# A decoder step on one Trainium2 core: one ones-matmul moved by one key tile, and the token operands of the mixing stage moved ahead on two engines

## The chip, the cores and the metric

The kernel runs on one core of one Trainium2 chip. A core has five engines with a queue of instructions each: TensorE (PE, matrix products, with its weight loads shown apart as PEld), VectorE (DVE), ScalarE (ACT), GpSimd (POOL) and SyncE (SP); here SP and POOL only issue transfers. The engines meet through semaphores. The metric is the device time of one execution in microseconds (us).

## The reference, cut to what matters

One layer of a decoder over 512 prompt tokens and 32 sample tokens (544 columns in the kernel), width 2048. Only the start of it is touched: the keys and values of 256 memory rows, and the normalised tokens that go into the combined projection `w_in`.

```python
def _rms(x, g):
    xf = x.astype(jnp.float32)
    y = xf * lax.rsqrt(jnp.mean(xf * xf, axis=-1, keepdims=True) + EPS)
    return (y * g.astype(jnp.float32)).astype(x.dtype)

def _mem_kv(mem, g_mem, w_k, w_v):
    m = _rms(mem, g_mem)
    k = (m @ w_k).reshape(Bn, N_MEM, N_XHEADS, XHEAD_DIM)
    v = (m @ w_v).reshape(Bn, N_MEM, N_XHEADS, XHEAD_DIM)
    return k, v
...
    h = _rms(x, norm_mix)
    proj = h @ w_in
    u = proj[..., :POOL_WIDTH]
...
```

Behind it come pooling and convolution, an output projection, cross-attention to the memory, a squared-ReLU MLP and a final normalisation.

## The kernel before

The order of the work is written out by hand, an instruction list for each engine. Every fp32 product is made of three products of rounded parts: an operand is rounded by ACT to its high part, DVE subtracts that from the original to get the low part, and PE adds high x high, high x low and low x high.

Weights come in **units** of 128 x 1024, through a ring of four slots. Unit n is loaded by SP into `unit_raw` as soon as DVE has split unit n-4 (L489), rounded by ACT into `unit_high` (L790, `convert`) when PE has used unit n-4, and split by DVE into `unit_low` (L1310, `convert`); PE waits for that split. So both converting engines run up to four units ahead of PE, and no further.

The stages around the change:

- **Key tiles** (L2165, `key_tile` on PE): 16 tiles of 128 key columns, t = 0 to 15, two units each, k0 to k31. DVE scales each finished tile into `temp` (L1382) and POOL stores it (L602). Beside them the tokens `residual` are squared: ACT makes the square (L804), DVE adds it to `square_sums` (L1320), one or two of the 16 slices beside each of the tiles 0 to 11, by the table `X_BY_KEY`. The code of DVE and ACT for tile t also converts units 2t+8 and 2t+9 of the run of k and v units, which wait for PE to use units 2t+4 and 2t+5: they run ahead of PE by those.
- **The sum of squares** (L2221, `sum_squares` on PE): four matmuls with a matrix of ones, when all 16 slices have been added. Before, it stands behind key tile 13 (`j == 1` of the last group of four, the 14th of the 16). From it DVE and ACT make `rstd` (`rstd_tokens`: L1326, the root on ACT L799, then three DVE steps L1331 to L1333).
- **Value units** (L2276): v0 to v31, twelve matmuls of 512 columns each. The loop number m = 0 to 27 in the code of ACT and DVE converts unit v(m+4). After v7, v15, v23 and v31 DVE scales two results (L1564).
- **Token operands**: the 16 slices of the tokens are handled in eight pairs, k = 0 to 7. For one pair DVE normalises two slices (L1434, `normalise_in`), ACT rounds their first halves (L850, `high_first`), DVE makes their low parts (L1405, `low_tokens`) and four sums and differences (`mix_tokens`, L1412 to L1420), ACT rounds two of these (`high_mixed`) and DVE makes the low parts (`low_mixed`). Before, the pairs stand beside the value units at m = 1, 4, 7, ..., 22, a whole pair at a time, with the mixed part of a pair one step later.
- **The combined projection** (L2300, `product_in`): 16 quads of seven products each, made of sums of weight blocks. The four blocks of quad 0 go into the ring's slots as v28 to v31 are split (SP, L501 to L507); DVE adds them (L1451, L1456, L1460, L1464), ACT rounds (L885), DVE splits (L1442). PE's product i of a quad waits, for i = 5, until ACT has copied partial result 3 (`copy_in`, L889).

Of the kernel before, what the change touches and what calls it, by code (L numbers as in the profile page):

```python
# [26 lines left out]
KT = D // P  # L27
# [4 lines left out]
CH = 8  # L32
# [53 lines left out]
START, TOTAL = starts()  # L86
# [102 lines left out]
def build(nc, weights, x_t, mem_t, params, cache_k, cache_v, pool_state, conv_state,  # L189
          y_t, k_t, v_out, pool_new, conv_new):  # L190
    ctx = ExitStack()
    with ctx:
# [592 lines left out]
        def _(act):  # L785
# [11 lines left out]
            def root(n, source, out):  # L797
                act.wait_ge(var_ready, n + 1)
                act.activation(out[:, 0:source.shape[1]], source, ACT.Abs_reciprocal_sqrt).then_inc(root_ready, 1)  # L799
# [39 lines left out]
            for t in range(KT):  # L839
# [4 lines left out]
                if t < KT - 2:  # L844
                    for n in (4, 5):
                        convert_next(unit("k_proj", 0, 2 * t + n))
            root(1, RSTD[:, :], ROOT_Y)

            def high_tokens(turn, i, k, source):
                act.activation(X7[i][:, k, 0, :], source, ACT.Copy).then_inc(tok_high[i], 1)  # L850
# [6 lines left out]
            def high_mixed(turn, k):  # L857

                for i, n in ((3, 1), (2, 3)):
                    act.wait_ge(tok_mixed, 4 * CH * turn + 4 * k + n)  # L860
                    high_tokens(turn, i, k, X7RAW[i][:, k, 1, :])
# [60 lines left out]
            def first_tap(g, r):  # L922
# [9 lines left out]
                act.activation(by_row(Y[:, c, SEQ:TOK]), own(Z[:, r, :], CPAD)[:, :, 0:DEC], ACT.Identity, scale=tap) \  # L932
                    .then_inc(tapped, 1)

            for i in range(4):
                for n in range(8):
                    m = 8 * i + n
                    if m < 28:
                        convert_next(unit("v_proj", 2 * i, n))
                    if m % 3 == 1 and m < 25:  # L940
                        k = m // 3
                        for p in (2 * k, 2 * k + 1):
                            high_first(MIX, p)
                        if k:
                            high_mixed(MIX, k - 1)
                    if m == 25:
                        high_mixed(MIX, CH - 1)
                    if m in (29, 30):
                        high_in(0, m - 29)
            high_in(0, 2)  # L950
# [352 lines left out]
        def _(dve):  # L1303
# [73 lines left out]
            def key_tile(t):  # L1377
                if t >= 2:

                    dve.wait_ge(k_stored[t % 2], 16 * (t // 2))  # L1380
                product(unit("k_proj", 0, 2 * t + 1))
                dve.tensor_tensor((TC, TD)[t % 2][:, 0:MEM], M[:, t % 4, 0:MEM], RSTDM[:, 0:MEM], ALU.mult) \  # L1382
                    .then_inc(psum_free, 1)
                if t == 0:
                    convert_next(unit("k_proj", 0, 3))
                for x in X_BY_KEY[t]:
                    add_squares(x, x + s0["squares"], SUMS, TOK)
                if t < KT - 2:
                    for n in (4, 5):
                        convert_next(unit("k_proj", 0, 2 * t + n))  # L1390

            for t in range(KT):
                key_tile(t)
            rstd_tokens(1, START["v_proj"]["squares"], ROOT_Y, ROOT_Z)

            for j in range(2):
                dve.wait_ge(k_stored[j], 16 * KT // 2)


            def b_block(j, l, k):  # L1400
                return X[:, CH * j + k, l * HALF:l * HALF + HALF]

# [29 lines left out]
            def normalise_in(p):  # L1432
                t = ORDER[p]
                dve.scalar_tensor_tensor(X[:, t, :], X[:, t, :], PAR[:, G_MIX + t:G_MIX + t + 1], RSTD[:, :],  # L1434
                                         ALU.mult, ALU.mult).then_inc(tok_normal, 1)

            def low_in(q, i):

# [116 lines left out]
            for i in range(4):  # L1555
                for n in range(8):
                    m = 8 * i + n
                    if n == 7:
                        product(unit("v_proj", 2 * i, 7))
                        for j in range(2):  # L1560
                            if i:

                                dve.wait_ge(v_stored[j], 16 * i)
                            dve.tensor_scalar((TC, TD)[j][:, 0:512], M[:, 2 * (i % 2) + j, 0:512],  # L1564
                                              RSTDM[:, MEM + j:MEM + j + 1], None, ALU.mult).then_inc(v_staged, 1)
                    if m < 28:
                        convert_next(unit("v_proj", 2 * i, n))
                    if m % 3 == 1 and m < 25:
                        k = m // 3
                        normalise_in(2 * k)  # L1570
                        normalise_in(2 * k + 1)
                        if k:
                            low_mixed(MIX, k - 1)
                        low_tokens(MIX, 0, k, k + 1, b_block(0, 0, k))
                        low_tokens(MIX, 1, k, k + 1, b_block(1, 0, k))
                        mix_tokens(MIX, k)
                    if m == 25:
                        low_mixed(MIX, CH - 1)
                    if m == 29:
                        sum_in_1(0)  # L1580
                        low_in(0, 0)
                    if m == 30:
                        sum_in_3(0)
                        low_in(0, 1)
                        sum_in_2(0)
# [571 lines left out]
        def _(pe):  # L2157
# [104 lines left out]
                    key_tile(i, j, False)  # L2262
            for j in range(4):
                key_tile(KT // 4 - 1, j, False)
                if j == 1:
                    sum_squares(1, START["v_proj"]["squares"])


# [494 lines left out]
```

## Time and profile before

| | us |
|---|---|
| median of 3 runs (lowest, highest) | 2620.81 (2619.9, 2622.91) |
| the profiled execution | 2623.57 |
| its span in the profile | 2621.9 |
| PE busy | 2573.2 (98%) |
| DVE busy | 1913.5 (73%) |
| ACT busy | 1105.8 (42%) |

The profiled execution is 2.76 us above the median; 1.67 us of it lie outside the span. The rows shown further below are times in that span. A timeline row gives the start in us, the duration, the engine, the line, the operation, what it writes and reads, how many were merged, and in brackets how long the engine sat idle before it and for whom. The row of a chain is a start, a duration and what ran.

### The profile page before, as it was taken

The page shows a single profiled execution, that of the slowest core. Times are in us where ns is not written, and L with a number is a line of the kernel's source. Part 1 is how long each engine was busy: PE and PEld are TensorE (multiplying, and loading weights), DVE is VectorE, ACT ScalarE, POOL GpSimd, SP SyncE. Part 2 cuts the span into 40 slices and gives each one's busy share as a digit, 9 for nine tenths or more (in the row PEclk, how much of TensorE's full clock was granted, in tenths as well). Part 3 has the DMA queues.
Part 4 walks back from the last instruction along what each step waited for, and adds up shares of the span by engine and source line. Part 5 has one row for each costly group of instructions (what it writes and reads, how often), then busy time and mean ns, then how long its engine had stood idle before and what let it go on. Part 6 is the DMA issues. An engine that isn't in the chain of part 4 may idle for free.

```text
span 2621.9 us, 47591 instructions
## 1 busy us (share of the span) xinstructions
PE 2573.2 (98%) x20056; PEld 2515.4 (96%) x20056; DVE 1913.5 (73%) x2342; ACT 1105.8 (42%) x1520; POOL 159.9 (6%) x253
## 2 busy tenths in 40 slices
PE   8999999999999999999999999999999999999997
PEld 8979999999999989989999999999999999999997
DVE  6688888773542244368988888888887888888888
ACT  6444444451331122134656555555543333333344
POOL 1000000010000000000011110000010000000000
PEclk9999999999999999999999999999999999999999
DMA  8653333362233445533466666555587555556542
GB/s 281 214 195 115 112 110 111 114 208 89 88 107 126 153 181 195 196 122 114 155 221 218 216 220 219 194 208 200 201 288 288 183 199 182 193 195 210 192 140 101
DMA packets 131856, 462.51 MB, mean 176 GB/s; under 512 B 11952, under 2 KB 18224, under 8 KB 120400
## 3 DMA queue, kind: packets, MB, share of 16 engines
q1 hardware_dynamic: 92448, 260.05, 30.3%
q0 software_dynamic: 39216, 199.71, 20.6%
q8 instruction: 144, 2.36, 0.4%
q14 instruction: 48, 0.39, 0.0%
HBM read 376.62 MB, written 83.09 MB: 175 GB/s over the span
## 4 chain that ended last, share of the span: by engine, by line
PE 88%; DVE 6%; issue 2%; ACT 2%; DMA 1%; SPq 0%; DVEq 0%; POOL 0%; ACTq 0%; POOLq 0%
PE psum_main L2555 27%; PE psum_main L2165 25%; PE psum_side L2555 20%; PE psum_main L2300 6%; PE psum_side L2300 4%; DVE unit_low L1310 1%; PE psum_main L2409 1%; PE psum_main L2481 1%; DVE unit_low L1843 1%; PE psum_side L2450 1%; PE psum_side L2374 1%; PE psum_main L2276 1%; DVE unit_low L1442 1%; DMA unit_raw<-weights 1%; DVE tokens L1405 0%
## 5 line engine op out<-in xcount | busy, mean ns | idle before, releaser
L1155 ACT ACTIVATE unit_high<-unit_raw 128x1024 fp32r<-128x1024 f32 x384 | 400.7, 1055 | 532.2 <-PE psum_main L2555 158.3
L1843 DVE TENSOR_TENSOR unit_low<-unit_raw,unit_high 128x1024 fp32r<-128x1024 f32 x384 | 468.1, 1222 | 109.1 <-ACT unit_high L1155 108.9
L2555 PE MATMUL psum_main<-tokens,unit_high 128*128 128x272 f32 x2048 | 388.5, 288 | 4.3 <-DVE hidden L1946 3.3
L2555 PE MATMUL psum_main<-hidden,unit_high 128*128 128x272 f32 x1984 | 377.1, 288 | 4.0 <-DVE residual L1976 2.7
L2165 PE MATMUL psum_main<-inner_a,unit_high 128*128 128x272 f32 x2080 | 348.1, 289 | 0.6 <-issue 0.6
L790 ACT ACTIVATE unit_high<-unit_raw 128x1024 fp32r<-128x1024 f32 x162 | 169.6, 1056 | 420.2 <-PE psum_main L2165 403.8
L2555 PEld LDWEIGHTS psum_main<-tokens,unit_high 128*128 128x128 f32 x2048 | 321.8, 189 | 5.2 <-DVE hidden L1946 4.0
L2555 PEld LDWEIGHTS psum_main<-hidden,unit_high 128*128 128x128 f32 x1984 | 312.2, 189 | 5.1 <-DVE residual L1976 3.7
L2165 PEld LDWEIGHTS psum_main<-inner_a,unit_high 128*128 128x128 f32 x2080 | 294.3, 188 | 3.8 <-issue 3.6
L2555 PE MATMUL psum_main<-tokens,unit_low 128*128 128x272 f32 x1024 | 295.0, 288 | 0.0
L2555 PE MATMUL psum_side<-tokens,unit_high 128*128 128x272 f32 x1536 | 293.1, 288 | 1.4 <-issue 0.8
L1310 DVE TENSOR_TENSOR unit_low<-unit_raw,unit_high 128x1024 fp32r<-128x1024 f32 x162 | 196.6, 1223 | 127.3 <-ACT unit_high L790 126.5
L2555 PE MATMUL psum_main<-hidden,unit_low 128*128 128x272 f32 x992 | 286.1, 288 | 0.0
L2555 PE MATMUL psum_side<-hidden,unit_high 128*128 128x272 f32 x1488 | 283.7, 288 | 0.2 <-DVE unit_low L1843 0.2
L2555 PEld LDWEIGHTS psum_side<-tokens,unit_high 128*128 128x128 f32 x1536 | 242.0, 189 | 2.0 <-issue 1.2
L2555 PEld LDWEIGHTS psum_side<-hidden,unit_high 128*128 128x128 f32 x1488 | 234.3, 189 | 0.6 <-issue 0.6
L2555 PE MATMUL psum_side<-tokens,unit_low 128*128 128x272 f32 x768 | 221.6, 288 | 0.0
L2165 PE MATMUL psum_main<-inner_a,unit_low 128*128 128x272 f32 x1040 | 214.7, 287 | 0.0
L2555 PE MATMUL psum_side<-hidden,unit_low 128*128 128x272 f32 x744 | 214.5, 288 | 0.0
L2300 PE MATMUL psum_main<-tokens,unit_high 128*128 128x272 f32 x1024 | 194.7, 288 | 4.0 <-DVE conv_gates L1486 4.0
L2555 PEld LDWEIGHTS psum_main<-tokens,unit_low 128*128 128x128 f32 x1024 | 192.4, 188 | 0.0
L2555 PEld LDWEIGHTS psum_main<-hidden,unit_low 128*128 128x128 f32 x992 | 186.4, 188 | 0.0
(285 smaller groups left out, 4699.0 us busy)
## 6 DMA issues: line engine op xcount, KB each, us to landing
unit_raw<-weights SPq DMA_DIRECT2D x442, 512.0 KB, 4.3
hidden<-hidden_kept POOLq DMA_DIRECT2D x56, 1088.0 KB, 6.2
hidden_kept<-hidden_staged POOLq DMA_DIRECT2D x31, 1904.0 KB, 7.4
unit_sum<-weights SPq DMA_DIRECT2D x40, 512.0 KB, 3.6
residual<-x_t POOLq DMA_DIRECT2D x16, 544.0 KB, 6.5
residual_kept<-residual POOLq DMA_DIRECT2D x32, 272.0 KB, 5.0
cache_ring_t<-cache_k POOLq DMA_DIRECT2D x8, 1024.0 KB, 7.8
cache_low_a<-cache_v POOLq DMA_DIRECT2D x8, 1024.0 KB, 10.6
```

What stands on the lines that cost most here:

```text
L790: act.activation(WHI[:, s, :], RAW[:, s, :], ACT.Copy).then_inc(high_ready, 1)
L1155: act.activation(WHI[:, slot, :], raw, ACT.Copy).then_inc(mlp_high, 1)
L1310: dve.tensor_tensor(WLO[:, s, :], RAW[:, s, :], WHI[:, s, :].bitcast(F32), ALU.subtract) \
L1442: dve.tensor_tensor(WLO[:, slot, :], raw, WHI[:, slot, :].bitcast(F32), ALU.subtract) \
L1843: dve.tensor_tensor(WLO[:, slot, :], raw, WHI[:, slot, :].bitcast(F32), ALU.subtract) \
L2165: ins = pe.matmul(out, weights_at(w), moving, start=first and n == 0, stop=last and n == len(passes) - 1)
L2276: ins = pe.matmul(M[:, 2 * i + mt, 0:512], MEMS[:, 2 * n + kk, part, mt * P:mt * P + P], w[:, u[1], kk * 512:kk * 512 + 512], start=(n + k ...
L2300: ins = pe.matmul(out, w[:, slot, cols], X7[i][:, k, part, :], start=start and k == 0 and n == 0, stop=k == CH - 1 and n == 2, skip_group_ ...
L2374: ins = pe.matmul(S[32 * j:32 * j + 32, 2 + h % 2, r * MEM:r * MEM + MEM], Q[:, HT * h + k, SEQ:TOK], key_place(at)[:, j, kk * MEM:kk * ME ...
L2409: ins = pe.matmul(M[:, p % 4, 0:MEM], Q[:, HT * h + dk, tt * P:tt * P + P], keys, start=dk == 0, stop=dk == HT - 1)
L2450: ins = pe.matmul(S[32 * i:32 * i + 32, 2 + r, :], PS[:, mt, r, 32 * i:32 * i + 32], value_place(g, m)[:, i, :], start=mt == 0, stop=mt == 1)
L2555: ins = pe.matmul(bank, w[:, slot, col:col + P], moving[:, k, part, :], start=start and k == 0 and n == 0, stop=k == kk - 1 and n == 2, sk ...
```

## The change

Three edits.

1. PE: the sum of squares stands behind key tile 12 (`j == 0`) instead of key tile 13.
2. DVE: `rstd` is made behind the code of key tile 13 instead of behind tile 15. Pair 0 follows the scaling of tile 14, pair 1 that of tile 15, both ahead of the conversion of v4. ACT: the roundings of pairs 0 and 1 stand ahead of the conversion of v4.
3. The pairs 2 to 7 stand at m = 0, 4, ..., 20 in two portions: normalising and the mixed low parts of the pair before at m, the low parts and `mix_tokens` at m + 2. On ACT the pair's rounding is at m. Pair 7's mixed part is at m = 24.

The diff's core:

```diff
@@ ACT
             for t in range(KT):
...
-            root(1, RSTD[:, :], ROOT_Y)
+                if t == KT - 3:
+                    root(1, RSTD[:, :], ROOT_Y)
...
+            for p in (0, 1):
+                high_first(MIX, p)
+            high_mixed(MIX, 0)
+            for p in (2, 3):
+                high_first(MIX, p)
             for i in range(4):
                 for n in range(8):
                     m = 8 * i + n
                     if m < 28:
                         convert_next(unit("v_proj", 2 * i, n))
-                    if m % 3 == 1 and m < 25:
-                        k = m // 3
+                    if m % 4 == 0 and m < 28:
+                        high_mixed(MIX, m // 4 + 1)
+                    if m % 4 == 0 and m < 24:
+                        k = m // 4 + 2
                         for p in (2 * k, 2 * k + 1):
                             high_first(MIX, p)
-                        if k:
-                            high_mixed(MIX, k - 1)
-                    if m == 25:
-                        high_mixed(MIX, CH - 1)
@@ DVE
+            def first_operands(k):
+                low_tokens(MIX, 0, k, k + 1, b_block(0, 0, k))
+                low_tokens(MIX, 1, k, k + 1, b_block(1, 0, k))
+                mix_tokens(MIX, k)
+
             for t in range(KT):
                 key_tile(t)
-            rstd_tokens(1, START["v_proj"]["squares"], ROOT_Y, ROOT_Z)
+                if t == KT - 3:
+                    rstd_tokens(1, START["v_proj"]["squares"], ROOT_Y, ROOT_Z)
+                if t >= KT - 2:
+                    k = t - (KT - 2)
+                    normalise_in(2 * k)
+                    normalise_in(2 * k + 1)
+                    if k:
+                        low_mixed(MIX, k - 1)
+                    first_operands(k)
...
-                    if m % 3 == 1 and m < 25:
-                        k = m // 3
+                    k = m // 4 + 2
+                    if m % 4 == 0 and m < 24:
                         normalise_in(2 * k)
                         normalise_in(2 * k + 1)
-                        if k:
-                            low_mixed(MIX, k - 1)
-                        low_tokens(MIX, 0, k, k + 1, b_block(0, 0, k))
-                        low_tokens(MIX, 1, k, k + 1, b_block(1, 0, k))
-                        mix_tokens(MIX, k)
-                    if m == 25:
+                        low_mixed(MIX, k - 1)
+                    if m % 4 == 2 and m < 24:
+                        first_operands(k)
+                    if m == 24:
                         low_mixed(MIX, CH - 1)
@@ PE
             for j in range(4):
                 key_tile(KT // 4 - 1, j, False)
-                if j == 1:
+                if j == 0:
                     sum_squares(1, START["v_proj"]["squares"])
```

What stands in a row on DVE around the start of the value units. The names: `unit_low` is a unit's split, `temp_64` and `temp_65` take key tiles with even and odd number, the lines have moved by a few. Before, from the last two splits of the key tiles' code (v2 and v3) on:

```order
L1310 TENSOR_TENSOR unit_low<-unit_raw,unit_high 128x1024 [waits high_ready] x2
L1382 TENSOR_TENSOR temp_64<-psum_main,rstd_mem 128x256 [waits units_used,k_stored_0]
L1382 TENSOR_TENSOR temp_65<-psum_main,rstd_mem 128x256 [waits units_used,k_stored_1]
L1326 TENSOR_SCALAR rstd<-psum_side 128x544 [waits sums_done,summed]
L1331 TENSOR_TENSOR root_z<-root_y 128x544 [waits root_ready,var_ready]
L1332 SCALAR_TENSOR_TENSOR root_z<-root_z,rstd 128x544 [waits dve_steps]
L1333 SCALAR_TENSOR_TENSOR rstd<-root_z,root_y 128x544 [waits dve_steps]
L1310 TENSOR_TENSOR unit_low<-unit_raw,unit_high 128x1024 [waits k_stored_1,high_ready,k_stored_0,dve_steps]
L1310 TENSOR_TENSOR unit_low<-unit_raw,unit_high 128x1024 [waits high_ready]
L1434 SCALAR_TENSOR_TENSOR residual<-residual,par,rstd 128x544 x2
L1405 TENSOR_TENSOR tokens_90<-residual,tokens_90 128x272 [waits tok_high_0]
```

Now, from the scaling of key tile 15 on (pair 0, from L1430 to L1416, stands ahead of it):

```order
L1386 TENSOR_TENSOR temp_65<-psum_main,rstd_mem 128x256 [waits units_used,k_stored_1]
L1430 SCALAR_TENSOR_TENSOR residual<-residual,par,rstd 128x544 x2
L1401 TENSOR_TENSOR tokens_93<-tokens_raw_100,tokens_93 128x272 [waits tok_high_3]
L1401 TENSOR_TENSOR tokens_92<-tokens_raw_99,tokens_92 128x272 [waits tok_high_2]
L1401 TENSOR_TENSOR tokens_90<-residual,tokens_90 128x272 [waits tok_high_0]
L1401 TENSOR_TENSOR tokens_91<-residual,tokens_91 128x272 [waits tok_high_1]
L1408 TENSOR_TENSOR tokens_raw_100<-residual 128x272 [waits tok_normal]
L1409 TENSOR_TENSOR residual<-residual 128x272
L1412 SCALAR_TENSOR_TENSOR tokens_raw_99<-residual 128x272 [waits tok_mixed]
L1416 SCALAR_TENSOR_TENSOR residual<-tokens_raw_99,residual 128x272 [waits tok_ready_1,tok_mixed]
L1314 TENSOR_TENSOR unit_low<-unit_raw,unit_high 128x1024 [waits high_ready,k_stored_1,k_stored_0]
L1430 SCALAR_TENSOR_TENSOR residual<-residual,par,rstd 128x544 x2
```

The split of v4 (the `unit_low` row that waits for both `k_stored`) stood ahead of every pair; now two pairs stand ahead of it.

On ACT, behind the root, before:

```order
L799 ACTIVATE root_y<-rstd 128x544 [waits var_ready]
L790 ACTIVATE unit_high<-unit_raw 128x1024 [waits raw_loaded_0,units_used]
L790 ACTIVATE unit_high<-unit_raw 128x1024 [waits raw_loaded_1,units_used]
L850 ACTIVATE tokens_90<-residual 128x272 [waits tok_normal]
L850 ACTIVATE tokens_91<-residual 128x272 [waits tok_normal]
```

and now:

```order
L799 ACTIVATE root_y<-rstd 128x544 [waits var_ready]
L851 ACTIVATE tokens_90<-residual 128x272 [waits tok_normal]
L851 ACTIVATE tokens_91<-residual 128x272 [waits tok_normal]
L851 ACTIVATE tokens_93<-tokens_raw_100 128x272 [waits tok_mixed]
L851 ACTIVATE tokens_92<-tokens_raw_99 128x272 [waits tok_mixed]
L851 ACTIVATE tokens_90<-residual 128x272 [waits tok_normal]
L851 ACTIVATE tokens_91<-residual 128x272 [waits tok_normal]
L790 ACTIVATE unit_high<-unit_raw 128x1024 [waits raw_loaded_0,units_used]
L851 ACTIVATE tokens_93<-tokens_raw_100 128x272 [waits tok_mixed]
L851 ACTIVATE tokens_92<-tokens_raw_99 128x272 [waits tok_mixed]
L851 ACTIVATE tokens_90<-residual 128x272 [waits tok_normal]
L851 ACTIVATE tokens_91<-residual 128x272 [waits tok_normal]
```

Six roundings that wait for DVE's pairs 0 and 1 have moved ahead of the rounding of v4, and the four behind it ahead of that of v5.

## Rows read from the trace of the kernel before

**Rows 1.** One stretch, the value units: start:end, length, busy us of each engine, clock, DMA.
```profile
110.50:204.50 94.00, 88.89 (x386) 71.50 (x385) 78.91 (x124) 43.15 (x64) 4.33 (x8) 1.00 0.56 189
```

**Rows 2.** Waits from 88 to 230 us: who waited for whom, total, times, longest.
```profile
PE psum_main L2276 <- DVE unit_low L1310: 5.1, 6, 1.6
...
PE psum_side L2300 <- ACT partial_in L889: 2.7, 1, 2.7
```

**Rows 3.** Chain of waits, 85 to 112 us: key tiles 14 and 15 on PE.
```profile
99.20 11.52 PE psum_main L2165 x96
```

**Rows 4.** Timeline, 92 to 99 us, engines mixed: tile 12's end, the last square, the sum.
```profile
92.56 1.06 ACT L790 ACTIVATE unit_high<-unit_raw 128x1024 fp32r<-128x1024 f32 x1 [1.82 <-PE psum_main L2165]
...
93.65 1.23 DVE L1310 TENSOR_TENSOR unit_low<-unit_raw,unit_high 128x1024 fp32r<-128x1024 f32 x1 [1.66 <-ACT unit_high L790]
...
95.13 0.72 DVE L1320 TENSOR_TENSOR square_sums<-square_sums,temp 128x544 f32<-128x544 f32 x1
...
98.12 1.08 PE L2221 MATMUL psum_side<-square_sums,par 128*128 128x272 f32 x4
```

**Rows 5.** Timeline, PE's first value matmul, then DVE up to v6's split.
```profile
110.54 0.40 PE L2276 MATMUL psum_main<-unit_high,mem_split 128*128 128x512 f32 x1
...
113.64 0.71 DVE L1326 TENSOR_SCALAR rstd<-psum_side 128x544 f32<-128x544 f32 x1
...
116.67 0.72 DVE L1333 SCALAR_TENSOR_TENSOR rstd<-root_z,root_y 128x544 f32<-128x544 f32 x1
117.89 2.36 DVE L1310 TENSOR_TENSOR unit_low<-unit_raw,unit_high 128x1024 fp32r<-128x1024 f32 x2 [0.49 <-DMA k_t<-temp]
120.17 1.47 DVE L1434 SCALAR_TENSOR_TENSOR residual<-residual,par,rstd 128x544 f32<-128x544 f32 x2
...
124.15 3.49 DVE L1310 TENSOR_TENSOR unit_low<-unit_raw,unit_high 128x1024 fp32r<-128x1024 f32 x3
```

**Rows 6.** Timeline, ACT, behind the second rounding of pair 0.
```profile
122.01 2.00 ACT L790 ACTIVATE unit_high<-unit_raw 128x1024 fp32r<-128x1024 f32 x2
```

**Rows 7.** Timeline, DVE, one whole pair (k = 3) between splits.
```profile
146.42 1.47 DVE L1434 SCALAR_TENSOR_TENSOR residual<-residual,par,rstd 128x544 f32<-128x544 f32 x2
148.72 0.79 DVE L1405 TENSOR_TENSOR tokens<-tokens_raw,tokens 128x272 fp32r<-128x272 f32 x2 [0.82 <-ACT tokens L850]
...
151.79 3.49 DVE L1310 TENSOR_TENSOR unit_low<-unit_raw,unit_high 128x1024 fp32r<-128x1024 f32 x3
```

**Rows 8.** Timeline: v23's scaling on DVE, v27's start and quad 0's on PE.
```profile
188.20 1.40 DVE L1564 TENSOR_SCALAR temp<-psum_main,rstd_mem 128x512 f32<-128x512 f32 x2
...
190.79 0.50 PE L2276 MATMUL psum_main<-unit_high,mem_split 128*128 128x512 f32 x1 [1.56 <-DVE unit_low L1310]
...
204.52 0.47 PE L2300 MATMUL psum_main<-tokens,unit_high 128*128 128x272 f32 x2
```

**Rows 9.** Timeline, DVE and SP, from v31's split to quad 0's first sum.
```profile
196.12 1.23 DVE L1310 TENSOR_TENSOR unit_low<-unit_raw,unit_high 128x1024 fp32r<-128x1024 f32 x1 [1.27 <-ACT unit_high L790]
197.37 0.33 SPq L507 DMA_DIRECT2D unit_raw<-weights  x1
...
202.04 1.22 DVE L1451 TENSOR_TENSOR unit_sum<-unit_raw 128x1024 f32<-128x1024 f32 x1 [4.70 <-DMA unit_raw<-weights]
```

**Rows 10.** Chain of waits, 203 to 232 us: quad 0's product 1, then products 4's end to 5.
```profile
207.74 3.01 PE psum_side L2300 x24
...
220.05 2.09 ACT tokens L850 x2
...
222.48 4.67 PE psum_side L2300 x24
```

**Rows 11.** Stretches, columns as rows 1: behind that wait, and from 1920 us.
```profile
222.20:225.60 3.40, 3.12 (x14) 3.12 (x15) 3.27 (x4) 2.12 (x3) 0.00 (x0) 0.50 0.51 154
...
1920.00:1924.00 4.00, 3.15 (x24) 2.92 (x24) 1.05 (x1) 1.06 (x1) 0.53 (x1) 1.00 1.05 391
```

**Rows 12.** Timeline, PE: the longest wait behind which the clock stayed full.
```profile
1919.88 0.52 PE L2555 MATMUL psum_main<-tokens,unit_high 128*128 128x272 f32 x2 [2.29 <-DVE hidden L1946]
```

More of the change, by code:

```diff
@@ L1390, in key_tile @@
                         convert_next(unit("k_proj", 0, 2 * t + n))
-            for t in range(KT):
-                key_tile(t)
-            rstd_tokens(1, START["v_proj"]["squares"], ROOT_Y, ROOT_Z)
-            for j in range(2):
-                dve.wait_ge(k_stored[j], 16 * KT // 2)
             def b_block(j, l, k):
@@ L1435, in normalise_in @@
                                          ALU.mult, ALU.mult).then_inc(tok_normal, 1)
+            def first_operands(k):
+                low_tokens(MIX, 0, k, k + 1, b_block(0, 0, k))
+                low_tokens(MIX, 1, k, k + 1, b_block(1, 0, k))
+                mix_tokens(MIX, k)
+            for t in range(KT):
+                key_tile(t)
+                if t == KT - 3:
[7 more added lines that the diff above has]
+                    first_operands(k)
+            for j in range(2):
+                dve.wait_ge(k_stored[j], 16 * KT // 2)
             def low_in(q, i):
```

## The prediction

> **What bounds the kernel now.** I read the table of busy times first: PE is busy 98% of the span, so the time is PE's work and its pauses, and an edit counts only where PE waits or where the clock of its array falls. Then the waits of PE beside the changed code. There are two kinds [rows 2]: six waits of the value units for DVE's splits, 5.1 us, and one wait of quad 0's product 5 for ACT, 2.7 us. Third, the stretch of the value units [rows 1]: of 94.0 us PE is busy 88.9 and DVE 78.9. DVE holds PE up there because its work comes in lumps. A pair takes DVE from 146.42 to 151.79 = 5.4 us, and the three splits that follow 3 x 1.14 = 3.4 (the spacing of the two splits that start at 117.89 and end for the pair at 120.17), together 8.8 [rows 5, 7]. PE needs three units in that time. One unit is 2.72 us: five of them run from 190.79 to 204.52, 13.73 us, of which a restart takes 0.1 [rows 8]. Three are 8.2, so DVE loses 0.6 us to PE at each pair, and PE pays once its lead is used up. The whole stage runs from 110.54 to 204.52, 94.0 us, against 32 x 2.72 = 87.0 of matmuls: 6.9 us are lost (5.1 as idle time, the rest as restarts and pipeline refill).
>
> **Edit 1, the sum of squares one tile earlier.** It is worth nothing where it is used: DVE takes it up at 113.64 [rows 5], 14 us after the matmuls at 98.12 [rows 4], because DVE comes to `rstd` only behind the split of v3, which waits for PE's last key unit. The edit puts `rstd` behind key tile 13's code, but that code ends with this very split, so it only jumps two scalings (0.33 us each).
> Its cost is a new wait. PE's sum waits until all 16 squares are added. Two key tiles take 11.52 us, one 5.76 [rows 3]. The sum starts at 98.12 behind tile 13, so tile 12 ends at 98.12 - 5.76 = 92.36. The last square is added at 95.13 + 0.72 = 95.85 [rows 4]. Can it come sooner? On DVE it stands behind a split that waits for ACT, and ACT's rounding waited for PE to finish tile 12 (92.56, released by PE) [rows 4]: rounding, split, the scaling of tile 11, the addition, a chain of 3.5 us that only starts when PE reaches the sum. So PE stands from 92.36 to about 95.9, **+3.5 us**. Before, tile 13 covered this chain. Behind the waiting sum stand tiles 13 to 15 and everything else on PE; nothing that DVE holds then can catch up for it, since PE is the bound there. Bounds: 3.4 and 3.7, it is read off four rows.
>
> **The clock behind a wait.** Behind the wait of 2.7 us the granted clock was 0.50 (1.2 instead of 2.4 GHz) from 222.2 to 225.6, and behind the wait of 2.29 us at 1919.88 it stayed 1.00 [rows 11, 12]. Product 5 took 4.67 us there, product 1 at full clock 3.01 [rows 10]: 1.7 us more, the restart included. A stall of 3.5 us is longer than the one that lost the clock, so I add **+1.7 us** behind the sum; the other end is 0.1 (restart alone).
> The Trainium skill (TensorE: Matmul & The Clock Gate, Part 1) speaks against this edit: the throttled state is the default and only activity releases it. By that rule every new idle stretch of this size costs PE time twice; the trace agrees in one of the two places shown.
>
> **Edit 2, two pairs ahead of v4.** Count from R = 0 at PE's first value matmul (110.54 before). PE has v0 to v3 split or nearly so and needs v4 at 4 x 2.72 = 10.9. Before, v4's split started at 117.89, R = 7.35, and ended at 8.6, in time [rows 5]. Now DVE does first: `rstd`, which started at 113.64 = R 3.10 and now starts two scalings earlier at 2.45; to its end 116.67 + 0.72 it takes 3.75: R 6.2. The scaling of tile 14, 0.33: 6.55. Pair 0, which took 120.17 to 124.15 = 4.0 [rows 5]: 10.55. The scaling of tile 15: 10.9. Pair 1 with pair 0's mixed part: a whole pair of 5.4, less the 0.82 that DVE waited for ACT [rows 7], since ACT now rounds pair 0's mixed part ahead of pair 1's: 15.4. The store of tile 15, which DVE also awaits (it ended at 117.89 before, 4.2 us after the scalings [rows 5]), is back by about 15.2 and hides beside that. Then v4's split, 1.2 us: R 16.65. PE stands from 10.9 to 16.65, **5.8 us**. Queued behind the pairs are the splits of v5 and v6 too. ACT rounds v5 only after pair 2's second rounding, about 1.85 us after pair 2's normalising starts (122.01 against 120.17 [rows 5, 6]). With pair 2 starting at 16.55 this is 18.4, the rounding 1.05, the split 1.2: v5 ready at 20.75. PE needs it at 16.65 + 2.72 = 19.4, and waits **1.3 us** more. The load of v8 goes out behind v4's split and is needed at R 27.5, far off.
> At v4 the clock falls too, by the same row; v4 then ends 1.6 later, at 21.0, but v5 was not ready before 20.75. The slow clock and the second wait lie over each other: only 0.3 us of it is new.
>
> **Edit 3, two portions per four units.** A step of four units now costs DVE four splits, 4.55, and a pair of 5.4, in which the 0.82 us of waiting for ACT stay (they now stand ahead of the split of m + 1): 9.9 us, plus half a scaling pair of 1.3 [rows 8] on average, 10.6, against PE's 10.9. So DVE no longer falls behind. I go through the tightest splits: v7 ready at 25.35, needed at 26.3; v9 at 30.6, needed 31.8; v11, behind the first scaling pair, at 36.5, needed 37.2; from there the lead grows. No wait after v5, with 0.7 us to spare at v11.
> The value stage thus loses 5.8 + 1.3 + 0.3 of clock = 7.4 us where it lost 6.9: **+0.5 us**. The gain of edit 3 is real, and edit 2 spends it.
>
> **Quad 0.** Its product 5 waited for ACT, which waited through a dense chain on DVE and ACT that starts with the landing of the fourth block: load at 197.37, behind v31's split, sum at 202.04 = 2.5 us before PE's 204.52 [rows 8, 9]. That split was late since v27's was (PE waited for it, 190.79 [rows 8]) and v31's load stands behind it. Now v27's split has some 2 us of lead, v31's rounding waits for PE's use of v27 instead, four units before the end: 10.9 - 0.2 - 1.05 - 1.25 = 8.4 us before the end, where it was 204.52 - 197.35 = 7.2. So the chain runs 1.2 us earlier against PE, the wait of 2.7 becomes 1.5: **-1.2 us**. A wait of 1.5 is below the 2.29 that left the clock full, so the slow stretch goes with it: **-1.6 us** (0.1 of restart stays).
>
> **Sum.** +3.5 + 1.7 + 0.5 - 1.2 - 1.6 = **+2.9 us**. Against the profiled execution of 2623.57 that is 2626.5. It ran 2.76 above the median of the three, so for the median I take 2620.81 + 2.9 = **2623.7 us**. A measurement of this kernel tells about 0.2%, 5.2 us, from no change.
>
> **Rivals.**
> A. The sum's stall does not cost the clock. For it: the stretch of 2.29 did not; against: 3.5 is more than 2.7. Then +1.3 (1.6 less): 2622.1.
> B. Quad 0 keeps its wait and its slow clock, since the fourth block lands no earlier against PE's end. This decides if v31's split ends less than 0.4 us earlier than now against the end (the wait then stays over 2.3). For it: the load of v31 shares the queue with quad 0's first blocks, and my lead of v27 is a small difference of long sums. Against: all of DVE's load is earlier now. It gives back 2.8: +5.7, 2626.5, slower by 0.22%.
> C. Neither new stall comes, and the change does what its order suggests: then the value stage has its 6.9 back and quad 0 another 2.8, -9.7: 2611.1. It needs the last square to be added before 92.4 and v4's split before R 10.9, against four rows and a backlog of 15.4 us in front of it. It would have to be that DVE is ahead by two key tiles, and its busy time beside them is low only because it waits for PE.
>
> **How the numbers follow.** The forecast 0.60, A 0.20, B 0.15, C 0.05. Around each lies some 1.5 us, as the three runs do (2619.9 to 2622.91). Faster by over 0.2% (below 2615.6): C, 0.05. Slower by over 0.2% (above 2626.05): most of B, 0.09, and the upper edge of the forecast, 0.05: 0.14. Within: 0.81. The range reaches from A's lower edge, 2619.5, to B's upper part, 2627.5; it leaves out C and the edges.
>
> **What would show it.** Behind key tile 12 a PE wait of 3.5 us for `square_sums`, and clock 0.50 behind it. A PE wait of 5.5 to 6 us for a split at the fifth value unit and one of about 1.2 at the sixth, none after. DVE's chain behind them without a gap. The wait for `partial_in` at quad 0 near 1.5 with clock 1.00. From quad 1 on every stretch as before. It is wrong if waits return at v11 or v15 (edit 3 too thin), or if the waits are there but the total falls.

## The result, and the profile after

The changed kernel takes 2626.87 us (median of 19 runs, 2624.96 to 2628.63), the kernel before 2621.82 us (19 runs, 2619.9 to 2625.57). The measured ratio is 1.0018, with a 95% interval of 1.0011 to 1.0024: 4.7 us slower, between 2.9 and 6.3 (the two medians differ by 5.05). The forecast was +2.9 and 2623.7 us, with a range of 2619.5 to 2627.5, so the time lies in the range, near its upper end. Of the 3.2 us between the forecast time and the measured one, 1.0 is the starting point: the kernel before has a median of 2621.82 in 19 runs, and the forecast was added to 2620.81, the median of three.

The profiled execution of the kernel after has a span of 2625.5 us against 2621.9. PE is busy 2574.1 us where it was 2573.2, so of 3.6 us some 2.7 are time in which PE stood still, and the rest is more time for the same matmuls. Three places differ.

**The sum of squares.** The first view is the timeline around the end of key tile 12 (start and duration in us, engine, line, operation, what it writes and reads, count, idle time before it and for whom). It answers to [rows 4]; lines have moved by a few.

```profile
91.07 1.06 ACT L790 ACTIVATE unit_high<-unit_raw 128x1024 fp32r<-128x1024 f32 x1 [1.82 <-PE psum_main L2180]
...
92.16 1.23 DVE L1314 TENSOR_TENSOR unit_low<-unit_raw,unit_high 128x1024 fp32r<-128x1024 f32 x1 [1.65 <-ACT unit_high L790]
93.30 0.42 DVE L1386 TENSOR_TENSOR temp<-psum_main,rstd_mem 128x256 f32<-128x256 f32 x1
93.63 0.72 DVE L1324 TENSOR_TENSOR square_sums<-square_sums,temp 128x544 f32<-128x544 f32 x1
...
94.40 1.52 PE L2236 MATMUL psum_side<-square_sums,par 128*128 128x272 f32 x4 [3.37 <-DVE square_sums L1324]
```

The chain rounding, split, scaling, addition starts when PE comes to the sum, and PE waits 3.37 us for it. The sum itself takes 1.52 us where it took 1.08. The stretch behind it (columns as in rows 1) and the start of the first value matmul:

```profile
94.40:97.80 3.40, 3.40 (x14) 3.10 (x15) 0.00 (x0) 0.00 (x0) 0.15 (x1) 0.61 0.69 193
```

```profile
114.22 0.40 PE L2291 MATMUL psum_main<-unit_high,mem_split 128*128 128x512 f32 x1
```

**The value units.** The waits from 88 to 236 us (who waited for whom, total, times, longest) answer to [rows 2]: where there were six waits of PE for splits, there is one, of about the same sum.

```profile
PE psum_main L2291 <- DVE unit_low L1314: 5.5, 1, 5.5
PE psum_side L2236 <- DVE square_sums L1324: 3.4, 1, 3.4
...
PE psum_main L2315 <- DVE pool_lines L1503: 1.0, 1, 1.0
...
PE psum_side L2315 <- ACT partial_in L890: 0.6, 1, 0.6
```

DVE ahead of that wait, in the timeline (answers to [rows 5]), then PE's restart:

```profile
116.65 0.72 DVE L1330 TENSOR_SCALAR rstd<-psum_side 128x544 f32<-128x544 f32 x1
...
120.78 1.47 DVE L1430 SCALAR_TENSOR_TENSOR residual<-residual,par,rstd 128x544 f32<-128x544 f32 x2
...
125.10 1.47 DVE L1430 SCALAR_TENSOR_TENSOR residual<-residual,par,rstd 128x544 f32<-128x544 f32 x2
...
129.55 1.22 DVE L1314 TENSOR_TENSOR unit_low<-unit_raw,unit_high 128x1024 fp32r<-128x1024 f32 x1
...
133.61 2.36 DVE L1314 TENSOR_TENSOR unit_low<-unit_raw,unit_high 128x1024 fp32r<-128x1024 f32 x2 [0.74 <-ACT unit_high L790]
```

```profile
130.82 0.80 PE L2291 MATMUL psum_main<-unit_high,mem_split 128*128 128x512 f32 x1 [5.54 <-DVE unit_low L1314]
```

DVE goes from `rstd` through pair 0 (120.78) and pair 1 (125.10) to v4's split at 129.55 almost without a gap. PE restarts at 130.82, 16.60 us behind the first value matmul. The clock in that stretch and over the whole stage:

```profile
130.80:135.40 4.60, 4.58 (x11) 3.61 (x12) 3.86 (x6) 3.64 (x5) 0.00 (x0) 0.50 0.36 114
...
114.20:209.60 95.40, 89.86 (x387) 73.86 (x386) 81.17 (x126) 44.49 (x64) 4.32 (x8) 0.96 0.56 186
```

**Quad 0.** It starts at 209.57, so the stage is 95.35 us long (93.98 before). Its product 5 waits 0.61 us instead of 2.69 and the clock stays full, but product 6 now waits too:

```profile
225.41 0.52 PE L2315 MATMUL psum_side<-tokens,unit_high 128*128 128x272 f32 x2 [0.61 <-ACT partial_in L890]
...
229.70 0.52 PE L2315 MATMUL psum_main<-tokens,unit_high 128*128 128x272 f32 x2 [1.01 <-DVE pool_lines L1503]
```

```profile
209.60:235.80 26.20, 24.57 (x193) 24.13 (x192) 23.68 (x27) 16.16 (x21) 3.75 (x7) 1.00 0.34 111
```

The ledger of the two traces, each length between two events that both have:

| stretch | before | after | difference | forecast |
|---|---|---|---|---|
| ACT's rounding at the end of tile 12 to first value matmul | 17.98 | 23.15 | +5.17 | +5.2 |
| first value matmul to quad 0 | 93.98 | 95.35 | +1.37 | +0.5 |
| quad 0: from its start over eight products | 28.47 | 26.24 | -2.23 | -2.8 |
| from there to the end of the span | 2388.9 | 2389.7 | +0.8 | 0 |

These make +5.1. The program up to tile 12 ran 1.5 us shorter in the trace after (92.56 against 91.07). That stretch moves without any change to it: the sum behind tile 13 starts at 98.12 in the kernel before and at 96.14 in run 4 below, whose instructions are the same up to there. The spans thus differ by only 3.6.

### The profile page after: what moved, and what is told of

Its sections match the earlier page's. It is cut to its first block, busy times and chain, and to the rows that moved or that the text cites. A ratio compares the mean times of both kernels' runs of the same rounds, so it can differ in the third digit from the quotient of the medians.

```text
span 2625.5 us, 47590 instructions
## 1 busy us (share of the span) xinstructions
PE 2574.1 (98%) x20056; PEld 2517.8 (96%) x20056; DVE 1913.4 (73%) x2342; ACT 1107.1 (42%) x1520; POOL 159.4 (6%) x253
## 4 chain that ended last, share of the span: by engine, by line
PE 88%; DVE 6%; issue 2%; DMA 2%; ACT 2%; SPq 0%; DVEq 0%; ACTq 0%
PE psum_main L2570 26%; PE psum_main L2180 25%; PE psum_side L2570 20%; PE psum_main L2315 6%; PE psum_side L2315 4%; PE psum_main L2291 3%; DMA unit_raw<-weights 1%; PE psum_main L2424 1%; PE psum_main L2496 1%; DVE unit_low L1858 1%; DVE unit_low L1459 1%; PE psum_side L2465 1%; PE psum_side L2389 1%; ACT unit_high L1159 1%; DVE tokens L1401 0%
```

## The experiments

All ratios are against the kernel before, run beside each kernel on the same chip. Times between events are from the traces, in us.

**1. The sum of squares back at its place.** The kernel after, edit 1 alone undone:

```diff
-                if j == 0:
+                if j == 1:
                     sum_squares(1, START["v_proj"]["squares"])
```

> The changed kernel with edit 1 undone: the sum of squares stands behind key tile 13 again, edits 2 and 3 stay. My theory: the sum's wait (3.4 us) and the slow clock behind it (1.7 us) are a cost of their own, and edits 2 and 3 nearly cancel (value units +1.4, quad 0 -2.3 in the trace of after). Expected against the kernel before: -1 us (between -2 and +0.5), no wait of PE for square_sums, the wait of about 5.5 us for v4's split still there with 6.8 us at half clock around it. Rival (the sum's wait is paid back later, since DVE gets further ahead in it, and the loss is that of the two pairs): +4 to +5 us, as the changed kernel.

Measured: 2621.5 us (11 runs), ratio 0.9996 (0.9987 to 1.0005). The wait is gone, the sum has its 1.08 us back, and the wait at v4 is what it was:

```profile
97.75 1.08 PE L2236 MATMUL psum_side<-square_sums,par 128*128 128x272 f32 x4
...
126.78 0.80 PE L2291 MATMUL psum_main<-unit_high,mem_split 128*128 128x512 f32 x1 [5.54 <-DVE unit_low L1314]
```

The value stage takes 94.96 and quad 0's eight products 26.66, against 93.98 and 28.47 before: +1.0 and -1.8. So edits 2 and 3 together come out at no difference that can be measured, and the whole loss goes with edit 1.

**2. The sum of squares alone.** The kernel before with edit 1 only (`j == 1` to `j == 0`).

> The kernel before with edit 1 alone: the sum of squares behind key tile 12. My theory: PE waits 3.4 us for the last square, the clock is at half for one stretch of 3.4 us behind it, +5.1 us against before, and the value stage is as before (94.0 us). Rival (paid back later): 0 to +2 us, with the value stage shorter than 94.0 by what the wait cost.

Measured: 2628.28 us (11 runs), ratio 1.0021 (1.0012 to 1.003): +5.5 us. The wait is the same to the hundredth, with a lowered clock behind it, and the value stage is unchanged at 93.99, with its six waits:

```profile
94.65 1.18 PE L2221 MATMUL psum_side<-square_sums,par 128*128 128x272 f32 x4 [3.37 <-DVE square_sums L1320]
```

```profile
94.60:98.00 3.40, 3.35 (x17) 3.20 (x18) 0.00 (x0) 0.00 (x0) 0.20 (x1) 0.72 0.64 198
114.40:208.40 94.00, 88.88 (x386) 71.66 (x386) 79.17 (x124) 43.01 (x64) 4.33 (x8) 1.00 0.55 189
```

Runs 1 and 2 are the two halves of the change, and their ratios put the loss in edit 1 (1.0021 x 0.9996 = 1.0017, against 1.0018 for the whole). The 3.4 us during which PE stands bring DVE no lead that the value stage could use: DVE stands too, since it waits for PE's key units.

**3. The last square one tile earlier.** The kernel after, with the table of squares changed so that slice 15 is added beside tile 10 and the sum behind tile 12 finds it done:

```diff
-X_BY_KEY = ((0, 1), (2,), (3, 4), (5,), (6, 7), (8,), (9, 10), (11,), (12,), (13,), (14,), (15,), (), (), (), ())
+X_BY_KEY = ((0, 1), (2,), (3, 4), (5,), (6, 7), (8,), (9, 10), (11,), (12,), (13,), (14, 15), (), (), (), (), ())
```

> The changed kernel with all three edits, but the table X_BY_KEY adds the last square beside key tile 10 instead of 11. My theory: the wait at the sum is for the last addition on DVE, which stands behind a conversion that needs PE's key tile 12. One tile earlier it is done at about 90.1 us, before tile 12 ends, so the wait and its slow clock go: time as with edit 1 undone, -1 us against before (-2 to +0.5). Rival (the sum at this place waits or costs for another reason, such as its own load of the ones or the PSUM bank): still +4 to +5 us.

Measured: 2621.22 us (11 runs), ratio 0.9994 (0.9985 to 1.0003). The sum stands behind tile 12 without a wait:

```profile
90.49 1.08 PE L2236 MATMUL psum_side<-square_sums,par 128*128 128x272 f32 x4
```

This run prices the clock by itself. The first value matmul here and in run 2:

```profile
108.67 0.40 PE L2291 MATMUL psum_main<-unit_high,mem_split 128*128 128x512 f32 x1
```

```profile
114.45 0.40 PE L2276 MATMUL psum_main<-unit_high,mem_split 128*128 128x512 f32 x1
```

From the sum's start to the first value matmul PE does the same work in three kernels' traces: 18.18 here (108.67 - 90.49), 19.82 in the kernel after (114.22 - 94.40) and 19.80 in run 2 (114.45 - 94.65). The slow stretch behind the wait costs 1.6 us, on top of the wait's 3.4. Without either, the earlier place of the sum is worth nothing, as the prediction said: DVE takes the sum up at the same point of its queue.

**4. ACT's order in the kernel before.** The kernel before, with ACT's rounding of the mixed part of pair k-1 put ahead of the roundings of pair k. DVE takes them up in that order, and waited 0.82 us in each pair [rows 7]. One swap, no instruction more or less:

```diff
                     if m % 3 == 1 and m < 25:
                         k = m // 3
-                        for p in (2 * k, 2 * k + 1):
-                            high_first(MIX, p)
                         if k:
                             high_mixed(MIX, k - 1)
+                        for p in (2 * k, 2 * k + 1):
+                            high_first(MIX, p)
```

> The kernel before with one swap on ACT: the rounding of a pair's mixed part stands ahead of the roundings of the next pair instead of behind them. DVE's order is untouched. It takes away the 0.8 us that DVE waits for ACT in each of seven pairs. My theory: DVE's backlog in the value stage is partly waiting: three splits and a pair then take 8.0 us against PE's 8.2, the losses of the value stage fall from 6.9 to between 1 and 2 us, the wait of quad 0 stays about as it is: -5 us against before (-4 to -7). Rival (the lumps themselves make PE wait, whatever their sum): less than -1.5 us, and waits for unit_low of over 1 us remain at three or more places.

Measured: 2616.25 us (8 runs), ratio 0.9974 (0.9964 to 0.9985): -6.8 us. One pair on DVE, then the stage:

```profile
142.54 1.47 DVE L1434 SCALAR_TENSOR_TENSOR residual<-residual,par,rstd 128x544 f32<-128x544 f32 x2
143.93 0.79 DVE L1405 TENSOR_TENSOR tokens<-tokens_raw,tokens 128x272 fp32r<-128x272 f32 x2
...
147.00 3.49 DVE L1310 TENSOR_TENSOR unit_low<-unit_raw,unit_high 128x1024 fp32r<-128x1024 f32 x3
```

```profile
108.60:196.10 87.50, 87.33 (x386) 71.80 (x385) 78.25 (x124) 43.73 (x64) 4.33 (x8) 1.00 0.59 202
```

A pair takes 4.46 us (142.54 to 147.00) instead of 5.37, and with three splits 7.9, below PE's 8.2 for three units. The stage falls from 93.98 to 87.57 and one wait of 0.17 is left. So 0.9 us of DVE per pair was all that stood between the kernel before and a stage that PE bounds. This confirms the reading that the stage loses its 6.9 us because DVE is too slow for each pair. The 0.6 us per pair of the prediction is too small a size for it: seven pairs make 4.2. The scalings, 1.3 us of DVE behind every eight units [rows 8], add about 0.5 us to each three units, which makes 1.1 per pair. In run 4 a pair with this share comes to an estimated 8.4 us, still 0.2 above PE's 8.2; that little, DVE's lead absorbs.

**5. v4 ahead of the pairs.** Run 1's kernel, with the conversion of v4 moved ahead of pair 0 on ACT and, on DVE, ahead of the scaling of tile 14 and so of both pairs; v5 stays behind them.

```diff
+            convert_next(unit("v_proj", 0, 0))
...
-                    if m < 28:
+                    if 0 < m < 28:
                         convert_next(unit("v_proj", 2 * i, n))
```

> The changed kernel with edit 1 undone and the conversion of v4 put ahead of the two pairs on ACT and DVE (right behind rstd on DVE). My theory: the loss at v4 is not that split's place but the backlog of DVE, two pairs of 4.0 and 4.6 us that start only after PE has begun the value units. The wait moves from v4 to v5: v4 ready at 8.5 us after PE's first value matmul (needed at 10.9), v5 at 20.7 (needed at 13.6), a wait of about 7 us, with half clock behind it. Value stage 95.5 to 96.5 us, time against before 0 to +1.5 us. Rival (v4's place is the fault, one conversion moved mends it): value stage under 90 us, -6 to -8 us.

Measured: 2622.91 us (11 runs), ratio 1.0 (0.9991 to 1.0009): no gain. The wait has moved by one unit and has grown by 1.4:

```profile
129.93 0.79 PE L2293 MATMUL psum_main<-unit_high,mem_split 128*128 128x512 f32 x1 [6.90 <-DVE unit_low L1315]
```

```profile
109.20:205.60 96.40, 89.50 (x386) 73.60 (x385) 81.35 (x125) 44.82 (x64) 4.34 (x8) 0.96 0.55 184
```

v4's split starts at 115.48, in time. Then come pair 0, pair 1 and pair 2's first portion, and v5's split starts at 128.65, for a need at 109.24 + 5 x 2.72 = 122.8. It is not v4 that is at fault but the amount of work in a row: whichever unit stands behind it pays.

**6. The pairs between the last splits of the key tiles' code.** From the kernel after: the sum behind tile 13 again, `rstd` behind the scaling of tile 12, pair 0 between the splits of v0 and v1, pair 1 behind that of v3, and the two portions as in edit 3. DVE idles in that stretch in the kernels before and after, since its splits wait there for PE. ACT gets the same order. DVE's part:

```diff
-            for t in range(KT):
+            for t in range(KT - 3):
                 key_tile(t)
...
+            rstd_tokens(1, START["v_proj"]["squares"], ROOT_Y, ROOT_Z)
+            convert_next(unit("k_proj", 0, 28))
+            key_tile(KT - 3)
+            normalise_in(0)
+            normalise_in(1)
+            first_operands(0)
+            for n in (29, 30, 31):
+                convert_next(unit("k_proj", 0, n))
+            normalise_in(2)
+            normalise_in(3)
+            low_mixed(MIX, 0)
+            first_operands(1)
+            for t in (KT - 2, KT - 1):
+                key_tile(t)
```

> What the change's words say, done where DVE is idle: the sum of squares behind key tile 13 as before; on DVE rstd stands behind the scaling of key tile 12 (ahead of the conversions of v0 to v3), pair 0 between those of v0 and v1, pair 1 behind that of v3; ACT in the same order; pairs 2 to 7 in two portions as in edit 3. My theory: rstd then starts about 10 us before PE's first value matmul, pair 1 is done at about 7.6 us after it, v4 is split at 9.4 (needed at 10.9), so no wait for a split remains and edit 3 shows what it is worth: value stage 87 to 87.6 us (94.0 before), quad 0 shorter by 2.3, -8 to -9.5 us against before. Rival (the portions do not hold by themselves, and the waits of after vanished only since PE had been held up at v4): waits for unit_low at v11 or v15, value stage over 89 us, -3 to -6 us.

Measured: 2617.18 us (9 runs), ratio 0.9976 (0.9967 to 0.9986), which is -6.3 us. Better than both kernels, but less than expected: the stage took 89.78 us, not the 87 to 87.6 that I looked for. DVE's rows show why:

```profile
118.34 0.75 DVE L1388 TENSOR_TENSOR temp<-psum_main,rstd_mem 128x256 f32<-128x256 f32 x2
121.74 1.22 DVE L1316 TENSOR_TENSOR unit_low<-unit_raw,unit_high 128x1024 fp32r<-128x1024 f32 x1 [2.65 <-DMA k_t<-temp]
```

Ahead of v4's split stands a wait for the stores of tiles 14 and 15, which protects two buffers that the split doesn't touch. In the kernel before it cost 0.49 us [rows 5], in the kernel after the pairs hid it. Here the scalings come last and it is exposed; two PE waits of 1.08 and 1.01 us follow, at v4 and v5.

**7. The wait for the stores where it is needed.** Run 6's kernel, with that wait moved to the first scaling of value results, the first instruction to write over the two buffers:

```diff
-            for j in range(2):
-                dve.wait_ge(k_stored[j], 16 * KT // 2)
...
                             if i:
                                 dve.wait_ge(v_stored[j], 16 * i)
+                            else:
+                                dve.wait_ge(k_stored[j], 16 * KT // 2)
```

> The kernel of the run before this one (sum behind tile 13, rstd behind tile 12's scaling, pairs 0 and 1 between the last splits of the key tiles' code, portions as in the change), with one thing moved: DVE's wait for the stores of key tiles 14 and 15 stands ahead of the first scaling of value results, which is the first to write over the two buffers, instead of ahead of v4's split. Nothing is left out. Theory (DVE's place in the queue is the cause: a split comes late when anything stands ahead of it, even a wait that the split doesn't need): in the run before, v4's split came at 121.74 after 2.65 us of waiting for the store, though its scaling chain was done at 119.09; the first value matmul stood at 110.87, so v4's split should now come at R = 8.2 and end at 9.4, ahead of PE's need at 10.9; v5 is split by R 13.4 against a need at 13.6; no PE wait at v4 and v5, the value stage 87.1 to 87.6 instead of 89.78, total 2.2 to 2.6 us below the run before: 2614.5 to 2615.5, ratio to before 0.9967 to 0.9972. Rival (the run before was held up by ACT's rounding of v5 and v6 behind pair 2, not by the store): the two waits of 1 us stay, the stage stays near 89.5, total 2617.

Measured: 2614.74 us (6 runs), ratio 0.9969 (0.9957 to 0.9981), the fastest of all.

```profile
116.34 0.75 DVE L1388 TENSOR_TENSOR temp<-psum_main,rstd_mem 128x256 f32<-128x256 f32 x2
117.00 1.22 DVE L1316 TENSOR_TENSOR unit_low<-unit_raw,unit_high 128x1024 fp32r<-128x1024 f32 x1
```

```profile
108.90:196.00 87.10, 87.10 (x387) 72.06 (x386) 75.95 (x115) 42.66 (x61) 4.33 (x8) 1.00 0.63 208
```

v4's split starts 8.13 us behind the first value matmul (117.00 - 108.87), and PE has no wait from there to quad 0: 87.12 us, which is the stage's floor (32 x 2.72 = 87.0). The step from run 6 is 2.7 us in the stage. The spans differ by 2.9 (2615.6 to 2612.7), but that they agree is luck: the part ahead of the value units is 2.0 shorter in this trace and the part behind quad 0's eight products 2.35 longer. By the medians the step is less certain, as the two intervals overlap.

## Why the prediction was right, and where its sizes were off

**The wait at the sum: right.** Forecast 3.5 (3.4 to 3.7), measured 3.37, twice. The four rows from which the chain was read were enough, and the reason why it could not come sooner (ACT's rounding is released by PE's own end of tile 12) is the first row of the profile after.

**The clock behind it: right.** Forecast 1.7, measured 1.6 by run 3, with clock 0.61 and 0.72 behind the wait in two traces. Rival A, that this stall would not cost the clock, had 0.20 and did not come. The Trainium skill (TensorE: Matmul & The Clock Gate, Part 1) says that the throttled state is the default and that activity releases it; the traces agree at this place (0.61 and 0.72). That every new idle stretch of this size costs twice, as the prediction read the rule, the kernel after does not bear out at its wait of 2.90 us near 1920, behind which the clock stayed at 1.00 (rows below).

**The value stage: the waits right, the clock too small.** v4's split was to be ready at 16.65 behind the first value matmul, and PE restarted at 16.60. v5's split was to be ready at 20.75, and the second of the rows of DVE's splits gives 133.61 + 1.22 - 114.22 = 20.6. The wait for v5 that the prediction named did not appear, because the slow clock lay over it entirely. The mis-sized term is the clock: I took 1.6 us, from a single slow stretch. In the trace after, the clock is at half for 6.8 us around this wait, from 129.25, while PE still stands, to 136.08. From 130.82 to 137.26 PE issues 17 matmuls, which at full clock take 17 x 0.227 = 3.9 us (a unit's 12 take 2.72) and here took 6.4: 2.6 us, where I had counted 1.3 for v5 and 0.3 for the clock. With 5.7 instead of 5.8 for v4's wait that is +0.9 us, the difference between +0.5 and +1.37. In run 3 a wait of the same length, 5.55, had a single slow stretch of 3.4 us, and the stage was 94.31, 1.0 shorter than that of the kernel after. The instructions of the stage are the same in both; why one trace has twice the slow time stays open.

**Edit 3: right.** No wait follows v5 in the kernel after, nor in runs 1, 3 and 5. The tight spot, v11, was to be ready at 36.5: its split starts at 149.40 and takes 1.22, 36.4 behind the first value matmul. Run 7 tests the 0.7 us to spare without PE being held up first: there v11's split ends 29.2 behind the first value matmul, for a need at 11 x 2.72 = 29.9, and PE doesn't wait. DVE's wait for ACT is there too, 0.74 us in each of the pairs 2 to 7. "Edit 2 spends what edit 3 gains" is what run 1 shows: +1.0 in the stage with both. Run 7, with edit 3's portions but without edit 2's lump, has no wait.

**Quad 0: the sign and nearly the size, by another sum.** The load of the fourth block was to come 8.4 us ahead of quad 0 instead of 7.2. The chain of the kernel after has it:

```profile
201.24 3.64 DMA unit_raw<-weights
...
204.97 1.23 DVE unit_sum L1468
```

209.57 - 201.24 = 8.33. The block also landed sooner: from its load to DVE's sum 3.73 us where it was 4.67 [rows 9]. Together that is 2.1 us, and the wait shrank by 2.1, not 1.2. Only the first half is the change's for sure. In all six kernels that have the two portions the load comes 8.33 ahead of quad 0 (7.15 to 7.34 in the other three), but it takes 3.6 to 4.4 us to land in the six, and their waits at product 5 range from 0.61 to 1.38. Why it landed sooner than before stays open. But the 1.6 us of slow clock were not there to be had. This was my mistake: I looked at which engine lost the time, not at what came next. Product 6 writes to `psum_main`, out of which DVE must first have made `pool_lines`. In both kernels DVE starts on that 3.7 us behind product 5's start, and PE starts product 6 soon after. Before, at half clock, and after, at full:

```profile
226.22 0.50 DVE L1486 SCALAR_TENSOR_TENSOR pool_lines<-psum_main,partial_in 128x240 f32<-128x240 f32 x2
...
226.98 0.41 PE L2300 MATMUL psum_main<-tokens,unit_high 128*128 128x272 f32 x2
```

```profile
229.14 0.50 DVE L1503 SCALAR_TENSOR_TENSOR pool_lines<-psum_main,partial_in 128x240 f32<-128x240 f32 x2
```

From product 5 to product 6 there are 4.50 us before (222.48 to 226.98) and 4.29 after (225.41 to 229.70). The slow clock cost 0.2, not 1.6, since PE would have stood in the same place waiting for DVE. Run 1 repeats it: 221.36 to 225.65, 4.29. Rival B, that quad 0 would keep its wait and its slow stretch, did not come either.

**The sum.** The forecast of +2.9 and the measured +4.7 (+5.1 in the two traces) differ by the clock at v4 (+0.9), by quad 0 (+0.6) and by the rest of the program (+0.8), which I had put at nothing. That last piece arises between 1919 and 1993 us, where PE has many short waits for `hidden`, for splits and for `residual`. The first is longer after (2.90 us against 2.29 [rows 12]), the next gives it back, and later ones take it again:

```profile
1924.32 0.49 PE L2555 MATMUL psum_main<-hidden,unit_high 128*128 128x272 f32 x2 [1.18 <-DVE unit_low L1843]
```

```profile
1926.82 0.49 PE L2570 MATMUL psum_main<-hidden,unit_high 128*128 128x272 f32 x2 [0.53 <-DVE unit_low L1858]
```

Nothing ties it to the change: from quad 0's eight products to its end the program takes 2388.9 us before, and in the eight other traces anything from 2387.9 (run 6) to 2390.6 (run 1), with 2389.7 in run 4, which is the kernel before with one swap. What moves it stays open.

By the number alone rival B, with +5.7, is nearer to the measured +4.7 than the forecast, and the median of 2626.87 lies above the 2626.05 from which the prediction counted a time as slower, with 0.14 for that. What speaks for the forecast and against B is the traces: the wait at quad 0 shrank and the slow stretch there went. The three misses and the starting point (1.0) all point one way and leave 0.6 us to the end of the range; that the time stayed inside is in part luck. Rival C, that the change would do what its order suggests, needed v4's split before 10.9; it came at 15.3 (129.55 - 114.22). Run 7 shows what it takes to get there: -8.1 us by its ratio, near the rival's -9.7.

## What to carry to other kernels

Moving work ahead in an engine's queue pays only where that engine idles. Add up everything that then stands in front of the next hand-over, and compare it with how far the consumer can run by itself (here four units, 10.9 us): work of 15 us in a row cost its excess at both places where it was tried (the kernel after and run 5), and the same work between splits that wait for PE anyway cost nothing (run 7). Before a consumer's early start is counted as a gain, look at its last producer. And before a slow stretch is counted as a loss, look at who is next in line: it may cost nothing.

## What was not expected of the hardware

Whether PE's clock falls behind a stall was not settled by the stall's length. The wait for `conv_gates` near 545 us is 1.88 us in all nine traces. In runs 1, 5 and 7 half clock follows it, in the other six not. The wait for `hidden` near 1915 us was 2.29, 2.30, 2.62 and 2.90 us in four traces (before, runs 6 and 4, after) that kept the full clock and 2.73, 2.79, 2.90, 2.95 and 2.98 in five (runs 1, 7, 3, 2, 5) that lost it. For each of the two waits, a trace with the full clock behind it and one without (the timeline's row, then the stretch that follows). Kernel after, where the stretch from 550.60 follows the wait of 1.88:

```profile
1923.03 0.51 PE L2570 MATMUL psum_main<-tokens,unit_high 128*128 128x272 f32 x2 [2.90 <-DVE hidden L1961]
```

```profile
1923.00:1926.40 3.40, 3.26 (x24) 3.04 (x24) 0.95 (x1) 1.06 (x1) 0.53 (x1) 1.00 1.07 389
...
550.60:554.00 3.40, 3.35 (x26) 3.36 (x27) 3.40 (x5) 0.83 (x2) 0.00 (x0) 1.00 0.36 88
```

Run 3:

```profile
1917.09 0.82 PE L2570 MATMUL psum_main<-tokens,unit_high 128*128 128x272 f32 x2 [2.90 <-DVE hidden L1961]
```

```profile
1917.00:1920.40 3.40, 3.31 (x15) 3.32 (x16) 0.90 (x2) 1.06 (x1) 0.53 (x1) 0.52 1.04 400
```

Run 7:

```profile
537.65 0.52 PE L2320 MATMUL psum_main<-tokens,unit_high 128*128 128x272 f32 x2 [1.88 <-DVE conv_gates L1506]
```

```profile
537.60:541.00 3.40, 3.35 (x16) 3.35 (x17) 3.40 (x5) 1.06 (x1) 0.00 (x0) 0.57 0.42 122
```

In the 3.4 us behind the same wait PE runs 24 matmuls or 15, and 26 or 16. Run 7 lost the clock at both places and is still the fastest. Whether the clock falls also differs between executions of one kernel: the mean granted clock of the nine of run 6 lies between 0.996 and 0.998, and one stretch of 3.4 us at half clock is worth about 0.0007 of it (1.7 of 2615 us). A forecast should give a stall of 2 to 3 us a chance of the slow stretch, not a yes or no. The stalls of 3.37 and 5.5 to 6.9 us lost the full clock in every trace that had them, and so did those of 2.45 to 2.69 us at quad 0 (before, runs 2 and 4).
